# VectorE and ScalarE take token sums and low parts one round later at three phase changes

## The reference

```python
x = x + 0.5 * swiglu(rms_norm(x, ffn1_norm), ffn1_w_gate, ffn1_w_up, ffn1_w_down)
proj = rms_norm(x, mix_norm) @ w_in          # z | x,B,C | dt | u
y_ssd = ssd_group(z, xbc, dt_raw, ...)       # conv, chunked scan over 64 frames, gated norm
y_pool = multiscale_pool_group(u, ...)       # trailing means over 2/4/8/16 frames
x = x + concat(y_ssd, y_pool) @ w_out
x = x + 0.5 * swiglu(rms_norm(x, ffn2_norm), ffn2_w_gate, ffn2_w_up, ffn2_w_down)
return rms_norm(x, final_norm)
# swiglu(h, g, u, d) = (silu(h @ g) * (h @ u)) @ d ; rms_norm divides by the root mean square, times a gain
```

## Time and profile before

| | |
|---|---|
| median of 3 runs | 1037.92 us (1037.42 to 1038.1) |
| profiled execution, its own time | 1038.42 us |
| its span | 1036.6 us |
| mean granted TensorE clock | 0.983 |
| busy: PE, DVE, ACT, POOL | 999.3, 781.8, 462.3, 212.0 us |
| HBM read, mean rate | 96.54 MB, 95 GB/s |

### The profile page before, as it was taken

One profiled execution on the slowest core, in us unless ns is written; L12 is line 12 of the kernel. 1 busy time (PEld: TensorE's weight loads), 2 busy tenths in 40 slices (PEclk: granted clock), 3 DMA queues, 4 the chain that ended last, 5 costly groups with the idle time before them and its releaser, 6 DMA issues. The chain is left out here.

```text
span 1036.6 us, 15358 instructions
## 1 busy us (share of the span) xinstructions
PE 999.3 (96%) x6118; PEld 878.2 (85%) x6118; DVE 781.8 (75%) x983; ACT 462.3 (45%) x603; POOL 212.0 (20%) x179
## 2 busy tenths in 40 slices
PE   9979999999999989999999999879999999999996
PEld 7879889998999658878787888759988999889975
DVE  5788568985697778787699796677966798567864
ACT  6455225552354446653234653344632455325532
POOL 1003002320031242321063452101110113001321
PEclk9989999999999989999999999979999999999998
DMA  8405313442232242322322233422252225412402
GB/s 270 138 24 158 104 41 110 136 143 82 61 103 62 64 125 84 94 65 78 82 82 68 75 89 95 122 82 82 83 162 82 82 82 153 134 41 85 119 21 82
DMA packets 188655, 99.63 MB, mean 96 GB/s; under 512 B 3524, under 2 KB 187944, under 8 KB 188584
## 3 DMA queue, kind: packets, MB, share of 16 engines
q1 hardware_dynamic: 187912, 97.60, 32.2%
q10 hardware_dynamic: 672, 1.05, 0.3%
HBM read 96.54 MB, written 2.10 MB: 95 GB/s over the span
## 5 line engine op out<-in xcount | busy, mean ns | idle before, releaser
L547 POOL TENSOR_TENSOR post<-post,rstd 128x256 f32<-128x256 f32 x57 | 93.3, 1637 | 536.5 <-DVE post L1062 536.5
L1601 PE MATMUL bank<-thi,w_hi_part 128*128 128x256 f32 x608 | 169.5, 279 | 5.8 <-DVE tlo L1023 3.6
L1602 PE MATMUL bank<-tlo,w_hi_part 128*128 128x256 f32 x608 | 168.9, 278 | 0.0
L1603 PE MATMUL bank<-thi,w_lo_part 128*128 128x256 f32 x608 | 168.7, 277 | 0.0
L1537 PE MATMUL bank<-xghi,w_hi_part 128*128 128x512 f32 x352 | 143.5, 408 | 10.4 <-DVE xglo L977 10.4
L972 DVE TENSOR_TENSOR w_lo_part<-w_raw,w_hi_part 128x1024 fp32r<-128x1024 f32 (+1 forms) x102 | 124.8, 1224 | 22.0 <-ACT w_hi_part L644 12.3
L1619 PE MATMUL bank<-acthi,w_hi_part 128*128 128x512 f32 x346 | 136.2, 394 | 4.4 <-DVE upd L1103 2.4
L1538 PE MATMUL bank<-xglo,w_hi_part 128*128 128x512 f32 x352 | 138.5, 393 | 0.0
L1539 PE MATMUL bank<-xghi,w_lo_part 128*128 128x512 f32 x352 | 138.4, 393 | 0.0
L1621 PE MATMUL bank<-acthi,w_lo_part 128*128 128x512 f32 x346 | 134.8, 390 | 0.0
L1620 PE MATMUL bank<-actlo,w_hi_part 128*128 128x512 f32 x346 | 134.7, 389 | 0.0
(11 more groups left out here) (260 smaller groups left out, 1958.1 us busy)
## 6 DMA issues: line engine op xcount, KB each, us to landing
w_raw<-in_ffn_w_gate SPq DMA_DIRECT2D x42, 512.0 KB, 3.7
w_raw<-in_ffn_w_up SPq DMA_DIRECT2D x42, 512.0 KB, 4.6
w_raw<-in_ffn_w_down SPq DMA_DIRECT2D x32, 512.0 KB, 4.4
w_raw<-in_w_in SPq DMA_DIRECT2D x29, 512.0 KB, 3.6
w_raw<-in_w_out SPq DMA_DIRECT2D x16, 512.0 KB, 3.9
w_raw<-in_ffn_w_down SPq DMA_DIRECT2D x16, 384.0 KB, 4.1
out<-xtok SPq DMA_DIRECT2D x4, 512.0 KB, 3.1
xload<-in_x SPq DMA_DIRECT2D x3, 512.0 KB, 6.7
```

The lines of the kernel that those rows point to most:

```text
L1601: pe.matmul(out, w, hi, start=opens and e == 0 and k == 0, stop=False, skip_group_check=True)
L1602: pe.matmul(out, w, lo, start=False, stop=False, skip_group_check=True)
L1603: mm = pe.matmul(out, wl, hi, start=False, stop=end, skip_group_check=True)
```

## The change

The steps of the token sums and of the split of x are spread over neighbouring rounds, at each of the three phase changes. TensorE's, GpSimd's and SyncE's lists are the same as before; VectorE's and ScalarE's hold the same instructions in another order (the small `neg_gain` is now made in two places).

1. The first two pairs of token sums are computed in the opening: `b12` of pairs 0 and 1 among the first tiles on ScalarE, `combine` 0 ahead of the reciprocal of the token norms and `combine` 1 between two weight conversions on VectorE. In the loop, `thi` and `tlo` of a pair come a round or more after its sums.
2. VectorE makes `xglo` of tile d - 1 behind the addition of tile d, no longer its own; ScalarE makes `xghi` ahead of the square.
3. ScalarE makes `xghi` and `b12` ahead of the square. VectorE, once it has added tile d, combines the pair of tile d - 1, and makes `xglo` of d behind that. `thi` comes behind the next conversion, and three of the four `tlo` move into the first direct units of the second stage.

```diff
@@ scalar, ffn @@
-                    if f == 0 and it.kind == "direct" and it.raw >= RING:
-                        halves_of_x(0, it.raw - RING, R_N1)
-                        combination_hi(0, it.raw - RING)
+                    if f == 0 and it.kind == "direct" and RING <= it.raw < RING + KH - 1:
+                        combination_hi(0, it.raw - RING + 1)
+                    if f and it.kind == "direct" and it.raw == 0:
+                        combination_hi(1, KH - 1)
@@ scalar, opening @@
             token_squares(0, 1)
+            halves_of_x(0, 0, R_N1)
...
             token_squares(2)
+            halves_of_x(0, 1, R_N1)
...
-            for m in (RING, RING + 1):
-                convert(m)
+            convert(RING)
+            combination_hi(0, 0)
+            halves_of_x(0, 2, R_N1)
+            convert(RING + 1)
+            halves_of_x(0, 3, R_N1)
 
             def last1(d):
+                norm_hi(1, d, R_MIX)
                 square(1, d, d % 2, xT[:, cols(d)])
-                norm_hi(1, d, R_MIX)
@@ scalar, output projection @@
             for d in range(DK):
-                square(2, d, d % 2, xT[:, cols(d)])
                 norm_hi(2, d, R_N2)
                 if d >= KH:
                     halves_of_x(1, d - KH, R_N2)
-                    combination_hi(1, d - KH)
+                square(2, d, d % 2, xT[:, cols(d)])
                 convert(M + U_OUTS + d + RING)
+                if d > KH:
+                    combination_hi(1, d - KH - 1)
@@ vector, ffn @@
                     if f == 0 and it.kind == "direct" and it.raw >= RING:
-                        combine(0, it.raw - RING, R_N1)
-                        combine_low(0, it.raw - RING)
+                        j = it.raw - RING
+                        if j == 0:
+                            combine(0, 2, R_N1)
+                        combine_low(0, j)
+                        if j == 1:
+                            combine(0, 3, R_N1)
+                    if f and it.kind == "direct" and it.raw:
+                        combine_low(1, it.raw)
@@ vector, opening @@
             first_lo_half(1, 1)
+            dve.wait_ge(neg_ready, 1)
+            combine(0, 0, R_N1)
             dve.wait_ge(std_ready, 1)
             dve.reciprocal(in_rms[:, 1, :], in_rms[:, 0, :]).then_inc(in_inv, 1)
...
-            for m in (RING, RING + 1):
-                convert(m)
+            convert(RING)
+            combine(0, 1, R_N1)
+            convert(RING + 1)
...
             def last1(d):
                 dve.tensor_tensor(xT[:, cols(d)], upd[:, d % 2, :], xT[:, cols(d)], ALU.add).then_inc(x_ready, 1)
-                norm_lo(1, d, R_MIX)
+                if d:
+                    norm_lo(1, d - 1, R_MIX)
 
             ffn(0, last1)
             update(0, 2, DK - 1, last1)
+            norm_lo(1, DK - 1, R_MIX)
@@ vector, output projection @@
                 dve.tensor_tensor(xT[:, cols(d)], PB[4 + d % 2][:, :], xT[:, cols(d)], ALU.add).then_inc(x_ready, 1)
+                if d == KH + 1:
+                    dve.wait_ge(neg_ready, 2)
+                if d > KH:
+                    combine(1, d - KH - 1, R_N2)
                 norm_lo(2, d, R_N2)
-                if d >= KH:
-                    combine(1, d - KH, R_N2)
                 convert(M + U_OUTS + d + RING)
-                if d >= KH:
-                    combine_low(1, d - KH)
+            combine(1, KH - 1, R_N2)
+            combine_low(1, 0)
             inverse(2)
```

More of the change, by code:

```diff
@@ L1199, in _ @@
             lows(2, 3)
+            dve.wait_ge(par_ready, 1)
+            dve.tensor_scalar(neg_gain[:, 0, :], par[:, R_N1:R_N1 + DK], -1.0, None, ALU.mult).then_inc(neg_ready, 1)
             shift(4, 5)
@@ L1219, in _ @@
             dve.wait_ge(par_ready, 2)
-            for f, gain in ((0, R_N1), (1, R_N2)):
-                dve.tensor_scalar(neg_gain[:, f, :], par[:, gain:gain + DK], -1.0, None, ALU.mult).then_inc(neg_ready, 1)
-            dve.wait_ge(neg_ready, 2)
+            dve.tensor_scalar(neg_gain[:, 1, :], par[:, R_N2:R_N2 + DK], -1.0, None, ALU.mult).then_inc(neg_ready, 1)
             def last1(d):
                 dve.tensor_tensor(xT[:, cols(d)], upd[:, d % 2, :], xT[:, cols(d)], ALU.add).then_inc(x_ready, 1)
-                norm_lo(1, d, R_MIX)
+                if d:
+                    norm_lo(1, d - 1, R_MIX)
             ffn(0, last1)
             update(0, 2, DK - 1, last1)
+            norm_lo(1, DK - 1, R_MIX)
             for m in (M_MIX + 2, M_MIX + 3):
```

## The result

| kernel | median us | runs, lowest to highest | profiled execution, us | its span |
|---|---|---|---|---|
| before | 1037.93 | 1037.42 to 1038.1 | 1038.42 | 1036.6 |
| changed | 1005.37 | 4 runs, 1004.9 to 1006.83 | 1006.83 | 1005.0 |

The ratio is 0.9691, 95% interval 0.9679 to 0.9703: 3.1% faster, 32.6 us by the medians. Forecast were 1005.0 us, in a range of 1002.5 to 1011. The profiled execution of the changed kernel is the slowest of its four, so what follows is made against its own span, 31.6 us shorter than that of before.

A forecast was written before the change was run, and what follows sets the result against it. TensorE was taken as the bound, with few waits, nearly all for `xglo` and `tlo`, plus slower clock behind them. Gains of 7.9 + 11.3 + 13.9 = 33.1 us from 1038.42 gave 1005.3, stated as 1005.0, range 1002.5 to 1011.

The forecast's parts named there:

- First change: Direct units to quads of the first stage: without TensorE's waits for `tlo`, `SUM2` starts at 62.5, 7.9 us less.
- The opening: Start of the kernel: two `combine` moved there cost VectorE 3.6 us, hidden by other work, so priced at 0.
- Term a: Down rounds before mixing: TensorE sets the pace at 4.08 us instead of 4.92, 3.9 us less.
- Term b: `dt_unit` to `stat`, first stage to mixing: `stat` starts at +4.5 instead of 9.6, 5.1 us less.
- rival 1: VectorE and GpSimd in each other's way, in rounds and ahead of each `stat`: 3 us, 1008; chance 0.12.
- a sign of being wrong: A new TensorE wait of over 1 us for `rstd`, a read bank or the sum of squares.
- Term c: Half-clock stretch from `stat`, first stage to mixing: 2.75 us instead of 5.05, 2.3 us less.
- Third change: Mixing to second stage: VectorE keeps up and the quads start at 688.6 instead of 702.47, 13.9 us less.
- my bounds of 4.2 and 5.5: VectorE's round, mixing to second stage: 4.2 us if `xglo` never met GpSimd, 5.5 with a whole addition in it.
- Rival 2: Mixing absorbs gains at the first phase change into mixing: at worst 7.4 us become bank waits, 1012.5; chance 0.08.
- Rival 3: Second stage's low parts come late and `SUM1` may stop: 5.8 us, 1011; chance 0.07.
- Rival 4: Clock falls to the low level under sustained TensorE load: 1055 at 100 us of low level; chance 0.02.

The follow-up runs named there:

- the last kernel above: Changed kernel with VectorE making the eighth addition of squares, and the reciprocal with its first bank reading ahead of the second weight conversion: 1004.50 us.
- The kernel in which VectorE adds: Changed kernel with the eighth addition of squares made by VectorE behind its last `xglo`, GpSimd's left out: 1006.88 us.

## Why the prediction was right, point by point

- **First change** (7.9 forecast, 7.99 in the profile, 8.3 alone): right. The four waits for `thi` and two `combine` are gone from the stretch. The last `tlo` ends at 57.5 and TensorE asks at 60.29, a margin of 2.8 us where I had said 1.2. Part of what I had missed is that VectorE, before, also stood idle for 0.91 us there, waiting for ScalarE's `b12`.
- **The opening** (0 forecast, 0.69 longer in the profiled execution): right, and the difference is not the change's. It is there already at ScalarE's second pair of `xghi`, ahead of any instruction that the change moves, and it comes and goes between kernels: that pair starts at 12.99 in the last kernel above, and at 13.60, latest of all, in the kernel with the third change alone, whose opening is that of before. In every profiled execution of this case `A11` starts 44.1 us after it, with the first change or without. What delays it stays open. ScalarE's timeline, first before:

```profile
12.59 1.33 ACT L661 ACTIVATE xghi<-xT,par 128x512 fp32r<-128x512 f32 x2 [2.19 <-DVE xT L1175]
```

And in the changed kernel, 0.70 us later:

```profile
13.29 1.34 ACT L661 ACTIVATE xghi<-xT,par 128x512 fp32r<-128x512 f32 x2 [2.88 <-DVE xT L1188]
```

- **Term a** (3.9, measured 4.02): right, rounds of 4.08 us. It needs VectorE's half of the change only.
- **Term b** (5.1, measured 4.13): the one term that was mis-sized. I put `stat` at +4.5 with GpSimd's addition at 1.30 us; it took 2.36, held behind VectorE's conversion, and `stat` started at +5.47. I had this as rival 1, with 1.2 us ahead of each of two `stat`. So the mechanism was on my list, and the forecast's own sum left it out. It came true at one of the two, at 1.07 us; at the second stage's `stat` (293.6 us after the first) TensorE has no wait. Without the addition on GpSimd `stat` starts at +3.82. TensorE's new wait of 1.61 us for the sum of squares is over the 1 us that I had named as a sign of being wrong: that sign came, for this term alone.
- **Term c** (2.3, measured 2.22): right, the half clock is gone.
- **Third change** (13.9, measured 13.91; 13.5 alone): right. VectorE's round has 4.97 us of work instead of my 4.8, because what meets GpSimd's addition is now the conversion (1.95 us) and no longer `xglo` (0.75). The round lies within my bounds of 4.2 and 5.5. VectorE and GpSimd in this round of the changed kernel:

```profile
645.30 0.75 DVE L984 SCALAR_TENSOR_TENSOR xglo<-xT,par,xghi 128x512 fp32r<-128x512 f32 x1
646.34 1.95 DVE L979 TENSOR_TENSOR w_lo_part<-w_raw,w_hi_part 128x1024 fp32r<-128x1024 f32 x1 [0.30 <-ACT w_hi_part L657]
...
645.51 1.69 POOL L535 TENSOR_TENSOR sumsq<-sumsq,sq 128x512 f32<-128x512 f32 x1 [3.75 <-ACT sq L668]
```

One reading of mine in this part was off: before, GpSimd's addition ended 0.5 us ahead of `xglo` (349.82 against 350.36), not 0.7. Nothing in the sum hangs on it.
- **Rival 2**, mixing absorbs the gain: false for the changed kernel, in which the reciprocal still waits 0.86 us for the square root. The kernel in which VectorE adds shows it: `stat` comes 1.65 us earlier there, and `sel` on GpSimd comes beside the two conversions ahead of the reciprocal.
- **Rival 3**, low parts late in the second stage: false; TensorE has no wait for `tlo` there. **Rival 4**, the clock under sustained load: false; the granted clock is 1.00 in every window from the start to 990 us, with TensorE 99% busy.

The sum was 1.5 us too large against the profiled execution: 1.0 of term b, 0.7 of the opening, and 0.2 the other way from the small terms. The median of the changed kernel lies 1.5 us below that execution, so the number came out closer (0.4 us) than its parts; that closeness is luck, and the second median of the same kernel was 1.6 us above the forecast. From the median before, the sum gives 1004.8, which I had written as 1005.0. I count the terms as the test, not the total.

## What to carry to other kernels

Where TensorE waits, look for an instruction in another engine's in-order queue that waits for a partner's result of the same round; take it one round later and the queue behind it moves up. Price the wait by the distance between two points of TensorE's timeline and not by its length, since the slower clock behind a long wait comes on top (2.95 us behind waits of 10.4). When a point has been moved up by microseconds, search at once for what is next there: here it was the order of three instructions, worth another 1.7 us, and a step that frees one path (`xghi` ahead of the square) cost 0.6 us on another.

## What the runs showed of the hardware

- VectorE and GpSimd hold each other up at SBUF by whole instructions, in both directions. VectorE's `xglo` (two inputs in SBUF) takes 0.75 us alone and 1.35 beside GpSimd's addition, a pair of conversions 2.35 and 3.42, GpSimd's addition 1.28 and 2.36. The Trainium skill, "SBUF — State Buffer", section "Who interferes with whom", says that the one that issues first blocks the other fully, and the runs agree. I had not expected that moving one square by 0.6 us would choose which of the two is held, nor that building masks on GpSimd (`sel`) is in it too: two conversions beside it took 4.16 us. Beside GpSimd's memsets, which only write, the pair keeps its 2.35 us (the kernel with VectorE's half alone, from 367.01 on).
- Products without use kept the granted clock at 1.00 through a wait of 8.4 us. The 30 products of 128 columns took 6.86 us; the last 1.77 us of the wait stayed idle and the clock still did not fall.
- TensorE, busy for 99% of 1005 us, kept its clock: 1.00 in every window up to 990 us.
